# An encoder trunk's dilated attention: the undilated group scored in natural query order over 256 keys, with a softmax of its own

## The reference

```
h    = rms_norm(x); proj = h @ w_in[l]                    # 1024 -> 5120, split into parts
ya   = banded_attention(rope(qa), rope(ka), va, 128, sink) # 8 query heads of 64, 2 key heads
for gi, (win, dil) in enumerate(((128, 1), (512, 4), (2048, 16))):   # 4 heads each
    o, lse = dilated_attention(rope(qg), rope(kg), vg, win, dil)
    # keys at offsets 0, +-dil, ... up to +-win/2; own softmax; lse = log of its denominator
wg   = softmax(stack(lses)); yb = sum(wg * stack(outs))    # the three groups mixed
x    = x + (sigmoid(gA) * (ya @ wa) + sigmoid(gB) * (yb @ wb)) @ w_out
x    = x + hier_moe(rms_norm(x))                           # 32 experts, 2 per token
```

## Time and profile before

| what | value |
|---|---|
| median of 3 runs | 1342.89 us (1341.87 to 1348.69) |
| profiled execution: its own time, its span | 1348.32 us, 1346.5 us |
| busy: TensorE, VectorE, ScalarE, GpSimd | 91%, 43%, 30%, 17% |
| chain that ended last, by engine | PE 61%, DMA 16%, DVE 9%, SyncE's queue 5%, ACT 4% |
| layer 0, T13 to the first branch projection | 76.23 us, TensorE busy 70.25 |
| the same of layer 1 | 77.19 us, TensorE busy 71.18 |

### The profile page before, as it was taken

How to read it: one execution, slowest core, us unless ns; L and a number is a source line. 1 busy time by engine, 2 the same in 40 slices (tenths; PEclk the granted TensorE clock), 3 DMA queues, 4 the chain that set the end, 5 groups by cost and what they waited for, 6 DMA issues and landing times.

```text
span 1346.5 us, 17162 instructions
## 1 busy us (share of the span) xinstructions
PE 1220.3 (91%) x6344; PEld 796.3 (59%) x6344; DVE 578.1 (43%) x1359; ACT 410.5 (30%) x768; POOL 234.2 (17%) x179
## 2 busy tenths in 40 slices
PE   6999989999998998889599999899999989988971
PEld 5777767888875443333177777678887844433320
DVE  5567676332344322222455767753332442222115
ACT  5334446343242110001334443563332411100002
POOL 0314140122201111111012322202221011111100
PEclk9999999999997999989899999899999979999996
DMA  5433221553656999999733333126537479999995
GB/s 212 118 100 87 79 79 32 176 199 109 224 201 211 381 426 423 424 422 412 311 91 94 95 95 93 33 67 204 170 106 297 159 260 406 422 424 423 420 412 211
DMA packets 69567, 306.62 MB, mean 228 GB/s; under 512 B 11969, under 2 KB 12225, under 8 KB 59249
## 3 DMA queue, kind: packets, MB, share of 16 engines
q1 hardware_dynamic: 58624, 282.45, 56.2%
q0 software_dynamic: 10720, 22.37, 4.5%
q10 hardware_dynamic: 144, 0.77, 0.2%
HBM read 290.34 MB, written 23.07 MB: 233 GB/s over the span
## 4 chain that ended last, share of the span: by engine, by line
PE 61%; DMA 16%; DVE 9%; SPq 5%; ACT 4%; issue 3%; DVEq 2%; POOLq 0%; ACTq 0%
PE bank L508 12%; PE bank L510 12%; PE bank L509 12%; DMA gu<-in_gu_w 12%; PE bank L792 11%; PE bank L808 4%; SPq L368 3%; DMA raw<-in_stream 2%; DVE prob L1293 2%; PE bank L648 2%; SPq L373 1%; PE bank L787 1%; DVEq L1270 1%; PE bank L618 1%; PE bank L735 1%
## 5 line engine op out<-in xcount | busy, mean ns | idle before, releaser
L792 PE MATMUL bank<-gu,xgt 128*64 128x512 f32 x1024 | 244.7, 629 | 38.8 <-DMA gu<-in_gu_w 37.0
L508 PE MATMUL bank<-h_hi,w_hi 128*128 128x512 f32 x640 | 253.3, 396 | 7.9 <-DVE w_lo L1173 3.8
L510 PE MATMUL bank<-h_hi,w_lo 128*128 128x512 f32 x640 | 249.5, 390 | 0.0
L509 PE MATMUL bank<-h_lo,w_hi 128*128 128x512 f32 x640 | 249.1, 389 | 0.0
L792 PEld LDWEIGHTS bank<-gu,xgt 128*64 128x64 f32 x1024 | 76.2, 145 | 203.7 <-issue 156.0
L1173 DVE TENSOR_TENSOR w_lo<-raw,w_hi 128x1024 fp32r<-128x1024 f32 x102 | 124.4, 1221 | 145.9 <-ACT w_hi L918 144.7
L508 PEld LDWEIGHTS bank<-h_hi,w_hi 128*128 128x128 f32 x640 | 120.2, 188 | 34.6 <-issue 8.1
L510 PEld LDWEIGHTS bank<-h_hi,w_lo 128*128 128x128 f32 x640 | 120.1, 188 | 25.6
L509 PEld LDWEIGHTS bank<-h_lo,w_hi 128*128 128x128 f32 x640 | 120.3, 188 | 23.7
L918 ACT ACTIVATE w_hi<-raw 128x1024 fp32r<-128x1024 f32 x102 | 107.5, 1054 | 59.7 <-PE bank L510 56.2
L808 PE MATMUL bank<-dn,zt 128*64 128x512 f32 x512 | 117.1, 599 | 6.3 <-ACT zt L1132 2.8
(11 more groups left out here) (173 smaller groups left out, 1595.1 us busy)
## 6 DMA issues: line engine op xcount, KB each, us to landing
gu<-in_gu_w SPq DMA_DIRECT2D x18, 4096.0 KB, 37.4
raw<-in_stream SPq DMA_DIRECT2D x112, 512.0 KB, 3.6
dn<-in_dn_w SPq DMA_DIRECT2D x18, 2048.0 KB, 34.3
gu<-in_gu_w SPq DMA_DIRECT2D x32, 1024.0 KB, 14.1
dn<-in_dn_w SPq DMA_DIRECT2D x20, 1024.0 KB, 19.0
gu<-in_gu_w SPq DMA_DIRECT2D x32, 512.0 KB, 4.9
swp<-pj SPq DMA_DIRECT2D x136, 64.0 KB, 2.3
dn<-in_dn_w SPq DMA_DIRECT2D x16, 512.0 KB, 5.7
```

The lines of the kernel that those rows point to most:

```text
L508: mm(dst, ah, bh, start=start, stop=False)
L509: mm(dst, ah, bl, start=False, stop=False)
L510: return mm(dst, al, bh, start=False, stop=stop)
L792: last = mm(bank[b][e * CAP:(e + 1) * CAP, :], xgt[:, x_s, k, e * CAP:(e + 1) * CAP], gu[w_s][:, e, k, :], start=k == 0, stop=k == KD - 1)
```

## The change

Group 0 leaves the shared softmax. In steps 16 to 23 each step still serves one query block of groups 1 and 2 in residue order, and now in the same step one block of 128 queries of group 0 in natural order. Its keys are 256: keys are kept in four chunks of 128 of which chunk 0 is the first 64 and the last 64 tokens and chunks 1 to 3 the runs between, so a block and 64 tokens on each side are two chunks. `qk_b` of group 0's queries is written in natural order by GpSimd, its value tile in chunk order by ScalarE.

- Scores: 256 near columns and 256 far columns a head, in one bank a head; three banks (0, 1, 2) in turn. Where the two chunks are not neighbours (blocks 0 and 3) the near part is two matmuls of 128 a head. The maxima are four instructions of 256 with results kept per group, without the joining minimum.
- Exponentials: four of 256 columns with four row sums. Normalise: one reciprocal of four, four scalings of 256.
- Transposes: 8 instead of 12, into banks 4 and 5; the copies are one of 512 by ScalarE and one of 512 by VectorE (before, three by ScalarE).
- Values: for each head two near calls into bank 7 and two far ones into bank 3, 8 calls instead of 12. A float32 matmul call stands as two instructions in the trace, so L648 shows x16 a step in place of x24; a transpose stands as one.
- New, once a layer: `logs` (ScalarE: logarithm of all sums, then an early sigmoid), `lse` (VectorE, two subtractions), `mix` (TensorE, twice: 16 calls that spread near minus far log-sums over the rows of a head), `near_weight` (ScalarE sigmoid), and `join`: VectorE (near - far) * weight + far, ScalarE `o_hi`, VectorE `o_lo`. `copy_o` of the dilated pairs becomes a far copy by ScalarE and a difference by VectorE.
- Order: every step is transpose(u), tile or turn, scores(u+2), values(u). Tiles stand in steps 0 to 12, 14, 16 and 18. The last block's rotary tiles come first, as tiles 15 to 20 (steps 7 to 12), its value tiles 21 to 23 after them; their turns are in steps 15, 17 and 19. Split 24 is in step 20, split 25 in step 21, the first gate and `logs`/`lse` in step 22; step 23 has the mixes, split 26 and join 0; join 1 and the second gate follow.
- The masks of group 0 are three of 256 columns instead of four of 512; five `held` semaphores become one.

The core of the diff:

```diff
+BLOCK_C = BLOCK_B[3:] + BLOCK_B[:3]
+BLOCKS = [BLOCK_A, BLOCK_B, BLOCK_C]
...
+FILLED = (*range(13), 14, 16, 18)
+NB = 2 * NSTEP_B
+CHUNKS = [(0, 1), (1, 2), (2, 3), (3, 0)]
+
+
+def score_bank(u, h):
+
+    if u < NSTEP_A:
+        return (2, 0, 1, 3)[2 * (u % 2) + h]
+    return (2 * (u - NSTEP_A) + h + 2) % 3
...
-    for u in range(NSTEP_A):
+    for u in range(STEPS):
         order.append(("transpose", u))
-        next_tile()
-        order.append(("scores", u + 2))
-        order.append(("values", u))
-    next_tile()
-    order.append(("scores", NSTEP_A + 2))
-
-    for u in range(NSTEP_A, STEPS):
-        order.append(("transpose", u))
-        if u > NSTEP_A:
-            order.append(("values", u - 1))
-        if u + 3 < STEPS:
-            order.append(("scores", u + 3))
+        if u in FILLED:
+            next_tile()
+        elif waiting:
+            order.append(("turn", waiting.pop(0)))
         if u == STEPS - 4:
             order.append(("split", NQ))
         if u == STEPS - 3:
-            order.append(("gate", 0))
-    order += [("values", STEPS - 1), ("gate", 1)]
+            order.append(("split", NQ + 1))
+        if u == STEPS - 2:
+            order += [("gate", 0), ("lse", 0)]
+        if u == STEPS - 1:
+            order += [("mix", 0), ("split", NQ + 2), ("mix", 1), ("join", 0)]
+        if u + 2 < STEPS:
+            order.append(("scores", u + 2))
+        order.append(("values", u))
+    order += [("join", 1), ("gate", 1)]
...
+        def chunk(ap, k):
+
+            if k:
+                return ap[:, k * P - 64:(k + 1) * P - 64]
+            return ap.rearrange("p (b n) -> p b n", n=64)[:, 0:8:7, :]
...
+                        if u > NSTEP_A:
+                            pe.wait_ge(mh_ok, l * NB + u - NSTEP_A)
+                        c0, c1 = CHUNKS[r]
+                        for n in ([None] if c0 and c1 else [0, 1]):
+                            for h in range(2):
+                                rows = slice(h * DH, (h + 1) * DH)
+                                dst = bank[score_bank(u, h)]
+                                if n is None:
+                                    mm(dst[:, 0:MG], qk[rows, 0, cols], qk[rows, 1, c0 * P - 64:(c1 + 1) * P - 64], start=True, stop=True)
+                                else:
+                                    mm(dst[:, n * P:(n + 1) * P], qk[rows, 0, cols], chunk(qk[rows, 1, :], CHUNKS[r][n]), start=True, stop=True)
...
+                def mix(p, l=l):
+
+                    if p == 0:
+                        pe.wait_ge(lse_ok, l + 1)
+                        pe.wait_ge(pj_act, (l + 1) * NQ)
+                        need(pe, mx_ok, (l + 1) * STEPS)
+                    dst = bank[6 if p == 0 else 2]
+                    for kind in range(2):
+                        for t in range(TT):
+                            for h in range(2):
+                                one = 4 * (p * NSTEP_B + t) + 2 * h + kind
+                                half = dst[h * DH:(h + 1) * DH, :]
+                                out = by_residue(half)[:, t, :, :] if kind else half[:, t * P:(t + 1) * P]
+                                last = mm(out, lse_b[:, one:one + 1].to_broadcast([P, DH]), ident, start=kind == 0 and t == 0,
+                                          stop=kind == 1 and t == TT - 1)
+                    last.then_inc(dm_ok, 1)
...
+                            for kind in range(2):
+                                p = prob[u % 3][:, h, kind * MG:(kind + 1) * MG]
+                                one = 4 * (u - NSTEP_A) + 2 * h + kind
+                                last = run(p, p, ACT.Exp, bias=max_b[:, one:one + 1], scale=-1.0, accum_out=sum_b[:, one:one + 1])
...
+                        run(by_residue(o_far[:, pair - 4, :]), in_order(bank[3][:, :]), ACT.Copy).then_inc(o12_ok, 1)
+
+                def logs(l=l):
+
+                    act.wait_ge(ex_ok, (l + 1) * STEPS)
+                    run(lse_b, sum_b, ACT.Ln).then_inc(ln_ok, 1)
+                    run(spare, ms[:, 0:1], ACT.Sigmoid)
+
+                def near_weight(p, l=l):
+                    act.wait_ge(dm_ok, l * 2 + p + 1)
+                    run(w_near[:, p, :], bank[6 if p == 0 else 2][:, :], ACT.Sigmoid).then_inc(wn_ok, 1)
+
+                def join(p, l=l):
+                    act.wait_ge(of_ok, l * 2 + p + 1)
+                    run(o_hi[:, 4 + p, :], o_near[:, p, :], ACT.Copy).then_inc(ohi_ok, 1)
...
+                            one = 4 * (u - NSTEP_A) + 2 * h
+                            src = bank[score_bank(u, h)]
+                            v.tensor_tensor_reduce(out=prob[u % 3][:, h, 0:MG], in0=src[:, 0:MG], in1=mask_b[:, (r + 1) // 2, :],
+                                                   scale=-SCALE, scalar=3.0e38, op0=ALU.add, op1=ALU.min, accum_out=max_b[:, one:one + 1])
+                            last = v.tensor_tensor_reduce(out=prob[u % 3][:, h, MG:MB], in0=src[:, MG:MB], in1=mask_b12[:, :],
+                                                          scale=-SCALE, scalar=3.0e38, op0=ALU.add, op1=ALU.min,
+                                                          accum_out=max_b[:, one + 1:one + 2])
+                            last.then_inc(mx_ok if h else mh_ok, 1)
...
+                        u0 = 4 * (u - NSTEP_A)
+                        v.reciprocal(den_b[:, 4 * s:4 * s + 4], sum_b[:, u0:u0 + 4])
+                        v.drain()
+                        for h in range(2):
+                            for kind in range(2):
+                                p = prob[u % 3][:, h, kind * MG:(kind + 1) * MG]
+                                last = ts(p, p, den_b[:, 4 * s + 2 * h + kind:4 * s + 2 * h + kind + 1], None, ALU.mult)
...
+                        dve.wait_ge(o12_ok, l * 2 + pair - 3)
+                        tt(o_near[:, pair - 4, :], bank[7][:, :], o_far[:, pair - 4, :], ALU.subtract).then_inc(od_ok, 1)
+
+                def lse(l=l):
+
+                    dve.wait_ge(ln_ok, l + 1)
+                    logs, tops = (a.rearrange("p (n k) -> p n k", k=2) for a in (lse_b, max_b))
+                    tt(logs[:, :, 0], logs[:, :, 0], tops[:, :, 0], ALU.subtract)
+                    tt(logs[:, :, 1], tops[:, :, 1], logs[:, :, 1], ALU.subtract).then_inc(lse_ok, 1)
+
+                def join(p, l=l):
+                    dve.wait_ge(wn_ok, l * 2 + p + 1)
+                    o = o_near[:, p, :]
+                    v.drain()
+                    tt(o, o, w_near[:, p, :], ALU.mult)
+                    v.drain()
+                    tt(o, o, o_far[:, p, :], ALU.add).then_inc(of_ok, 1)
+                    dve.wait_ge(ohi_ok, l * 6 + 4 + p + 1)
+                    tt(o_lo[:, 4 + p, :], o, o_hi[:, 4 + p, :].bitcast(FP32), ALU.subtract).then_inc(olo_ok, 1)
```

208 lines of the change are left out of this document (90 added, 118 removed).

## The result

Run in turn on one chip, the kernel before took 1344.32 us (median of 8 runs, 1341.37 to 1348.69) and the kernel after 1355.08 us (median of 8, 1351.76 to 1357.16): ratio 1.0080, 95% interval 1.0065 to 1.0096. The change makes it slower by 0.8%. The profiled execution took 1352.63 us (span 1350.5), 4.3 above that of before. The traces can therefore account for 4 us, not for all of the difference.

A forecast was written before the change was run, and what follows sets the result against it. TensorE, busy 91% of the span, was taken to bound the kernel. Steps +5.8, moved work -1.0 and clock +3.0 gave +7.8 us on the median 1342.89, so 1350.7; range 1326 to 1363.

The forecast's parts named there:

- forecast 2: Serial VectorE-ScalarE loop in six steps without a tile takes back what TensorE saves: 1350.7 us, chance 0.5.
- step 14: Tile step: transposes and tile 6.3, scores 1.04, values 0.81, together 8.15 us.
- steps 20 and 21: Steps without a tile: 7.7 us, plus 1.0 for the clock, and 6.3 us with a split and the loop.
- TensorE's part: Dilated steps: 1.35 us less each, about 11 a layer; net of both mixes, 7 us less TensorE work per layer.
- The loop: Dilated steps: maxima 1.45, exponentials 2.1, normalise 1.5, in series with hand-overs, 5.1 us against today's 4.42.
- The join: Step 22 to the branch: mixes, weights and join end at 20.4 us; the branch waits 1.1 for them.
- What is moved: Block C's reordered tiles: fewer turns in steps 8 to 10 against slower scalings, -0.5 us a layer, -1.0 in all.
- what I gave back for VectorE's scalings: Steps 8 and 9: scalings slow beside GpSimd's rotary work and a split waits, +1.1 us.
- The clock: Lower clock after TensorE gaps: 0.5 us for step 13, 1.0 for step 20; 1.5 a layer, +3.0 in all.
- Total: Whole kernel: +5.8 - 1.0 + 3.0 = +7.8 us, 1350.7 on the median of the runs.
- that TensorE stays the bound: Rival: loop closes under TensorE's work, 11 to 12 us a layer less, 1320; half-way about 1333; chance 0.25.
- That the clock falls in every gap: Rival: gaps after 13, 15, 17, 20, 21 leave next tile or gate at 1.2 GHz, +16, 1367; chance 0.18.

The follow-up runs named there:

- experiment 5: Kernel before, arithmetic unchanged, with only block C's rotary tiles first and its value tiles last: 1348.56 us, ratio 1.0019.
- experiment 9: Kernel after, all tiles in steps 0-15, late steps' scores early and values late, values 15 before scores 17, mixes and join 0 behind gate 0: 1332.76 us.
- Experiment 4: Kernel before, arithmetic unchanged, dilated steps with scores two steps ahead instead of three and each step's own values in the step: 1369.41 us, ratio 1.0181.
- Experiment 8: Kernel after, scores early and values late: in steps 19-21 with step 13 filler, 1353.34 us; in steps 16-21 with all tiles in 0-15, 1341.33 us.
- Experiment 3: Kernel after without logarithms, mixes, weights and join, output being near minus far: 1349.99 us, ratio 1.0037.
- experiment 6: Kernel after with three unread float32 calls on TensorE in each of the gaps of steps 13 and 20: 1352.66 us, ratio 1.0055.
- experiment 7: Kernel after, first: scores ahead of transposes in steps 19-21, ScalarE copying before exponentials, 1355.30 us; second: also split, then scores ahead of tiles 14, 16, 18, 1356.23 us.

## Why the prediction was right, point by point

The forecast was 1350.7 us, the time 1355.1, inside the range; the sign and the mechanism (forecast 2, the serial loop takes back what TensorE saves) hold. The fit of the sum below is in part luck: step 14 was 0.8 to 1.0 us longer than forecast and steps 20 and 21 together 1.7 shorter.

| Step | predicted | layer 0 | layer 1 |
|---|---|---|---|
| 13 | 5.7 + 0.5 clock | 6.30 | 6.32 |
| 14 | 8.15 | 9.14 | 8.92 |
| 15 | 4.25 | 4.38 | 4.37 |
| 16 | 8.8 | 8.77 | 8.77 |
| 17 | 5.0 | 4.64 | 4.65 |
| 18 | 8.8 | 8.61 | 8.62 |
| 19 | 4.4 | 4.63 | 4.63 |
| 20 | 7.7 + 1.0 clock | 7.49 | 7.72 |
| 21 | 6.3 | 5.77 | 5.54 |
| 22 to branch | 20.4 | 20.46 | 20.45 |
| Sum | 81.0 | 80.19 | 79.99 |

- **TensorE's part**: 7 us less a layer forecast. The busy time fell by 3.45 and 4.52, with the slow stretches in both numbers. Stretches with a granted clock of 1.00 compare better: 70.04 and 70.03 with the old arithmetic (experiment 5), 63.51 with the new (experiment 9, layer 1), 6.5 less. The two mixes take 3.71 us, against 3.9.
- **The loop**: right in place and size. Priced at 5.1 us, it takes 5.0 from the first of the maxima to the last scaling. Steps 15, 17 and 19 took 4.4 to 4.6 us, with VectorE waiting for the exponentials for 1.80, 1.20 and 0.88 us where I had put some 1.5 to 2. Experiment 4 shows the order as the cause: with the old arithmetic and the new order the step goes from 4.42 to 5.55. Experiment 8 shows it from the other side: with the new arithmetic and another order it is 3.3 to 3.5.
- **The join**: predicted at 20.4 with a wait of 1.1; it is 20.46 with 1.65. Experiment 3 prices it at 4.4 us a layer less 1.7 for work that then falls elsewhere.
- **What is moved**: -0.5 a layer forecast, -1.0 and -0.9 measured between T0 and T13 (102.39 and 103.32, against 103.39 and 104.25). Experiment 5 shows that the tiles' order alone does not bring this, so the right sign had only part of its reason. The turns that fall away in steps 8 to 10 bring 1.3 and 0.9 us in the kernel after (1.6 forecast); what I gave back for VectorE's scalings, 1.1, in steps 8 and 9, comes back in step 12 (1.0 and 1.3); and the rest, 0.6 and 1.5 us in steps 4 and 5, I did not foresee.
- **The clock**: +1.5 a layer. Beside the kernel with the filler (experiment 6) steps 13 and 14 lose 1.3 to 1.5 us; step 20's gap, where I placed 1.0, costs nothing in all. Step 14 is the term that I had too small (8.15 for 9.14 and 8.92): I put the loss into step 13 (0.5, measured 0.6), and the larger part, 0.95 and 0.73 us, falls into the tile behind the gap. That the clock term came out near its size with step 20's 1.0 missing is luck.
- **Total**: the sum of the traces is +7.0 in the attention and -1.9 in steps 0 to 12, +5.1, where I had +7.8. The medians say +10.8. The rest, 5 to 6 us, stands in no stretch that I compared: the two profiled executions lie on opposite sides of their medians. Two things in the other traces bear on it. Outside the stretches from T0 to the branch the fourteen profiled executions took 980.9 to 987.8 us, in no order that follows the changes, so a pair of traces cannot place a few us there. And the profiled execution of the kernel after has a short step 13: in the kernel of experiment 3 and the first of experiment 7, whose order is the same up to step 14, steps 13 and 14 together took 16.3, 19.8, 16.6 and 15.7 us, against 15.4 and 15.2 in it. In the longest of the four VectorE's split and product stood beside GpSimd's rotary sum and took 2.29 and 2.39 us instead of 1.21 and 0.68. By the mean of the four that would be 3.5 us for both layers; that it fills the difference of the medians is not shown.
- **Rivals**: that TensorE stays the bound fell with the order as written, but experiment 9 shows its price was real: 1320 and, half-way, 1333 were forecast for it, and 1332.8 was reached by another order, with a stretch of 71.2 and 69.6 us, where the 1320 needed 65. That the clock falls in every gap fell too: steps 15 to 19 and both gates run at 1.00 in the kernel after. Its first case came, smaller: the tile behind step 13's gap lost 0.95 and 0.73 us, not 2.8. It did come in experiments 7 and 8 (0.83, and 1.97 us for eight transposes), there in the gate, as that rival had it.

The Trainium skill, TensorE: Matmul & The Clock Gate, section "HAM oscillation", says that a loop whose waits outlast its matmuls starts each pass cold. The traces agree behind gaps of 3.34, 3.71 and 4.57 us; steps 15, 17 and 19 of the kernel after, with 0.9 to 1.4 us idle, show a clock of 1.00.

## What to carry to other kernels

Before work is taken from the engine that bounds, write down for one step the order of each in-order queue and the chain that closes from one step to the next; if a producer and its consumer both stand between two passes of the bounding engine, their sum is the new step. Here the lighter arithmetic made the loop 0.5 us shorter, and another order, with the scores one step earlier and the values one step later, took the step from 4.4 to 4.6 us down to 3.3 to 3.5. Moving an entry in a list that several engines share moves all of their parts: for each engine ask what now stands behind it, as the copy behind the exponentials, or the low part of a split behind a high part behind the exponentials. Before the arithmetic of a slower kernel of this kind is given up, its order is worth another look: here the same arithmetic runs from 1.027 to 0.990 of the kernel before.

## What the runs showed of the hardware

- A logarithm right behind exponentials cost a table load of its own, and the sigmoid behind it another:

```profile
233.56 1.28 ACT L1066 ACT_TABLE_LOAD   x1
...
235.10 1.28 ACT L1067 ACT_TABLE_LOAD   x1
```

Both lie under the first gate here. The Trainium skill, ScalarE: Activation LUTs, section "What ACT_TABLE_LOAD costs", gives about 1283 ns for the load itself and 2.66 us with a drain. The trace agrees on the load, 1.28 us, and shows no time for a drain: the logarithm starts at 234.85, 1.29 us behind the load's start.

- 2.84 us of matmuls that nobody reads, in a gap that was there anyway, made that step and the next together 1.3 to 1.5 us shorter (experiment 6).
- A gap of 2.53 us, behind one of 1.79, was enough for the lower clock in experiment 7: TensorE's next eight transposes took 1.97 us.

```profile
220.56 1.09 PE L678 MATMUL bank<-pt,v_b 128*64 128x128 f32 x16 [1.79 <-DVE pt L1363]
...
226.30 1.15 PE L678 MATMUL bank<-pt,v_b 128*64 128x128 f32 x16 [2.53 <-DVE pt L1363]
227.51 1.97 PE L649 MATMUL bank<-cst,prob 128*128 128x128 f32 x8
```

- The length of a gap alone did not decide it. The kernel of experiment 6 has the same gaps in both layers ahead of step 22 (0.96, 0.82 and 2.03 us), and the next eight transposes took 1.09 us in layer 0 and 1.87 in layer 1. Behind gaps of 1.75 and 2.30 us eight transposes took 1.97 us in the kernel before (layer 0, step 17); behind gaps of 1.16 and 2.30 they took 1.06 in the kernel of experiment 5 (step 16). A forecast should give such a drop a chance beside its price.
